# Rewriting the prologue of a hybrid attention block: raw memory rows transposed, loads in homes of their own, norm weight read from PSUM

## What is computed

```
hn    = rmsnorm(x, g_norm)                     # (1024, 1024)
proj  = hn @ w_in                              # columns aq ak av ag bq bk bv bg mq mg
a_out = sliding-window attention with sinks (aq, ak, av)
b_out = rmsnorm(differential attention (bq, bk, bv, lambda), subln_g) * (1 - lam_init)
memn  = rmsnorm(mem, g_mem)                    # (256, 1024)
kv    = memn @ w_mem_kv                        # 4 heads of keys, 4 of values
m_out = attention of mq over kv
h     = x + concat(a_out*silu(ag), b_out*silu(bg), m_out*silu(mg)) @ w_out
y     = rmsnorm(h, g_final)
```

## Time and profile before

| | us |
|---|---|
| median of 3 runs | 725.78 (725.2 to 725.81) |
| the profiled execution, device time | 726.04 |
| its span in the trace | 724.2 |

### The profile page before, as it was taken

How to read it: one execution, slowest core, us unless ns; L and a number is a source line. 1 busy time by engine, 2 the same in 40 slices (tenths; PEclk the granted TensorE clock), 3 DMA queues, 4 the chain that set the end, 5 groups by cost and what they waited for, 6 DMA issues and landing times.

```text
span 724.2 us, 11962 instructions
## 1 busy us (share of the span) xinstructions
PE 710.4 (98%) x3908; PEld 593.9 (82%) x3908; DVE 427.7 (59%) x916; ACT 311.9 (43%) x720; POOL 236.3 (33%) x204
## 2 busy tenths in 40 slices
PE   7999999999999999999999999999999999999996
PEld 7888788888888888888888888888888887888885
DVE  5884345776774577768357776835776686422231
ACT  5771333545544354554434545443454563212210
POOL 3564132324423232442323244232324452322210
PEclk9999999999999999999999999999999999999999
DMA  8663121111024101102400110241130266514211
GB/s 266 205 192 72 29 59 31 30 30 31 1 97 106 29 29 29 29 0 93 110 29 29 29 29 0 91 113 30 30 96 25 63 196 201 170 58 123 72 62 41
DMA packets 79400, 53.56 MB, mean 74 GB/s; under 512 B 36096, under 2 KB 71936, under 8 KB 79360
## 3 DMA queue, kind: packets, MB, share of 16 engines
q1 hardware_dynamic: 79360, 53.10, 25.6%
HBM read 44.18 MB, written 8.91 MB: 73 GB/s over the span
## 4 chain that ended last, share of the span: by engine, by line
PE 88%; issue 4%; DVE 2%; POOL 2%; ACT 1%; DMA 1%; SPq 0%; DVEq 0%; POOLq 0%; ACTq 0%
PE acc L1316 18%; PE acc L1317 17%; PE acc L1318 17%; PE score L1316 3%; PE score L1317 3%; PE score L1318 3%; PE score L1444 3%; PE trans L1317 3%; PE trans L1316 3%; PE trans L1318 3%; PE score L1446 3%; PE trans L1465 2%; POOL w_lo L815 2%; PE score L1522 2%; PE mixo L1317 2%
## 5 line engine op out<-in xcount | busy, mean ns | idle before, releaser
L1316 PE MATMUL acc<-x_hi,w_hi 128*128 128x512 f32 x544 | 216.3, 398 | 0.1
L1317 PE MATMUL acc<-x_lo,w_hi 128*128 128x512 f32 x544 | 212.5, 391 | 0.0
L1318 PE MATMUL acc<-x_hi,w_lo 128*128 128x512 f32 x544 | 212.2, 390 | 0.0
L815 POOL TENSOR_TENSOR w_lo<-w_raw,w_hi 128x512 fp32r<-128x512 f32 x86 | 113.8, 1345 | 190.3 <-ACT w_hi L555 190.3
L1318 PEld LDWEIGHTS acc<-x_hi,w_lo 128*128 128x128 f32 x544 | 102.1, 188 | 22.2
L1316 PEld LDWEIGHTS acc<-x_hi,w_hi 128*128 128x128 f32 x544 | 102.3, 188 | 21.5 <-issue 1.8
L1317 PEld LDWEIGHTS acc<-x_lo,w_hi 128*128 128x128 f32 x544 | 102.4, 188 | 18.2
L672 ACT ACTIVATE logits<-logits,stats_b 128x256 f32<-128x256 f32 (+3 forms) x64 | 52.6, 824 | 46.8 <-DVE stats_b L1121 46.8
L1113 DVE CUSTOM_DVE_ANT_0 logits<-score,b_bias 128x512 f32<-128x512 f32 (+1 forms) x96 | 53.8, 599 | 22.1 <-PE score L1446 19.2
L555 ACT ACTIVATE w_hi<-w_raw 128x512 fp32r<-128x512 f32 x86 | 49.4, 624 | 27.4 <-PE acc L1318 20.0
L681 ACT ACTIVATE p_hi<-trans 128x512 fp32r<-128x512 f32 x56 | 32.5, 595 | 63.2 <-PE trans L1465 38.9
(11 more groups left out here) (191 smaller groups left out, 1340.9 us busy)
## 6 DMA issues: line engine op xcount, KB each, us to landing
w_raw<-in_w_in SPq DMA_DIRECT2D x68, 256.0 KB, 3.4
mixed<-gates SPq DMA_DIRECT2D x9, 512.0 KB, 4.3
mix_raw<-mixed SPq DMA_DIRECT2D x8, 576.0 KB, 5.6
w_raw<-in_w_mem_kv SPq DMA_DIRECT2D x16, 256.0 KB, 4.0
logits<-in_x SPq DMA_DIRECT2D x8, 512.0 KB, 4.6
wo_raw<-in_w_out SPq DMA_DIRECT2D x8, 512.0 KB, 6.5
x_res<-in_x SPq DMA_DIRECT2D x8, 512.0 KB, 3.4
out_y<-y_row SPq DMA_DIRECT2D x16, 256.0 KB, 2.1
```

What stands on the lines that cost most here:

```text
L815: last = pool.tensor_tensor(w_lo[:, slot, cols], w_raw[:, slot, cols], w_hi[:, slot, cols].bitcast(F32), ALU.subtract)
L1316: pe.matmul(out, a_hi, b_hi, start=start, stop=False, skip_group_check=True)
L1317: pe.matmul(out, a_hi, b_lo, start=False, stop=False, skip_group_check=True)
L1318: return pe.matmul(out, a_lo, b_hi, start=False, stop=stop, skip_group_check=True)
```

## The change

All of it lies in the prologue; the head loop and the end are as before.

- The memory rows are no longer scaled before they are transposed. TensorE transposes them raw (8 + 8 transposes). The norm weight is applied when the transposed banks are split, where it is one number per partition (ScalarE with a scale column, VectorE L964 becoming a multiply-and-subtract, 8 operations of 256 columns each). The rows' 1/rms is applied when the products come out of PSUM: `mem_tile` multiplies by mem_rstd, which is made by two 128-wide ScalarE operations, two transposes and one copy.
- Norm weights: two DMAs of 8 rows x 512 B instead of two spread ones of 512 KB. g_mem is transposed into columns (gain_cols). g_norm is spread to all partitions in PSUM by 8 matmuls in plain float32 with a picking matrix, into two banks (gain_spread), and stays there.
- x rows are scaled in place, in pairs of blocks, as two 512-column halves per block that read the weight from PSUM. The Newton step's operations all have one tensor operand and column scalars; before, two of the five had two tensor operands.
- Homes: 8 for x blocks, 8 for memory weight tiles (two in w_raw, two in a_v, four in the upper 256 columns of x_hi and x_lo). So SP issues, with no wait but a short one on a memset, the memory, the weights' rows, tiles 0 to 7 and x blocks 0 to 5 in one stream, in the order t0 t1 t2 x0 t3 x1 t4 x2 t5 x3 t6 x4 t7 x5, then tiles 8 and 9, x6, x7, the constants.
- Weight halves: GpSimd signals each half (`w_lo_half`), and VectorE makes the first half of tile 0. TensorE begins a tile on its first half.
- Four PSUM banks for memory products and, in part, for transpositions, where there were two. Transposes come in groups of 4 between products: none until tile 4, then 4 after each tile, the rest among tiles 8 and 9, which run in the order 8 left, 9 left, 8 right, 9 right.
- The products that nobody reads shrink from 32 + 16 + 12 to 14 + 2 + 2.
- The table work on a_bias and b_bias moves from the end of the prologue to its start.

```diff
-BUSY = (32, ((0, 512), (8, 512), (16, 512), (32, 512)), ((64, 512), (0, 516), (0, 576)))
+BUSY = (14, 2, 2)
...
 @@ SP
             sp.dma_start(mem_raw[0][:, :], mem_rows[:, 0, :]).then_inc(mem_full[0], 16)
-            sp.dma_start(g_mem_b[:, :], g_mem.partition_broadcast(P)[:, 0, :]).then_inc(gmem_full, 16)
             sp.dma_start(mem_raw[1][:, :], mem_rows[:, 1, :]).then_inc(mem_full[1], 16)
...
+            for n in range(3):
+                load_mem_tile(n)
+            for t in range(5):
+                load_row(t)
+                load_mem_tile(t + 3)
+            load_row(5)
+            sp.wait_ge(w_lo_first, 1)
+            for par, col in enumerate((AV, AK)):
+                sp.wait_ge(w_lo_done, 1 + par)
+                load_tile(w_in_v, par, col, None)
+            load_row(6)
+            load_row(7)
...
 @@ ACT, in this order
+            row_squares(mem_raw[0][:, :], 0, mem_full[0])
+            mem_bank_hi(0)
+            w_hi_half(0, 0)
+            mem_bank_hi(1)
+            w_hi_half(0, 1)
+            mem_bank_hi(2)
+            mem_bank_hi(3)
+            split_hi(1)
+            row_squares(mem_raw[1][:, :], 1, mem_full[1])
+            pair_std(0)
+            split_hi(2)
+            spread_mem_rstd()
+            row_squares(x_raw[0], 2, rows_full[0])
+            split_hi(3)
...
 @@ DVE
+                        last = dve.scalar_tensor_tensor(out=row[:, cols], in0=row[:, cols],
+                                                        scalar=row_stats[:, 2 * pair + n + 2, 6:7],
+                                                        in1=gain_spread[s], op0=ALU.mult, op1=ALU.mult)
...
+            def mem_tile(n):
+                dve.wait_ge(acc_full, n + 1)
+                out = mk_raw[:, n // 2, :] if n % 2 == 0 else mv_t[:, (n // 2) * MEM:(n // 2 + 1) * MEM]
+                dve.tensor_tensor(out, pre_acc[n % 4][:, 0:MEM], mem_rstd, ALU.mult).then_inc(acc_free, 1)
...
+            for n in range(3):
+                mem_tile(n)
+            normalise(0)
+            mem_tile(3)
+            mem_tile(4)
+            for b in range(2):
+                x_bank_lo(0, b)
+            normalise(1)
+            mem_tile(5)
+            for b in range(2, 4):
+                x_bank_lo(0, b)
+            mem_tile(6)
+            for b in range(2):
+                x_bank_lo(1, b)
+            mem_tile(7)
+            for b in range(2, 4):
+                x_bank_lo(1, b)
+            normalise(2)
+            normalise(3)
...
 @@ PE
+            for n in range(MEM_TILES):
+                mem_tile(n)
+                if n == 1:
+                    pe.wait_ge(mem_spread_made, 1)
+                    for par in range(2):
+                        last = pe.transpose(trans[:, 0, par * P:(par + 1) * P], mem_spread[:, par, :], ident[:, :])
+                    last.then_inc(mem_rstd_turned, 1)
+                if n >= 4:
+                    pair, half = divmod(n - 4, 2)
+                    for b in range(2 * half, 2 * half + 2):
+                        spread_rows(pair, b)
...
+            shared_half(8, 0, range(KT))
+            for b in range(2):
+                spread_rows(2, b)
+            shared_half(9, 0, first)
+            for b in range(2, 4):
+                spread_rows(2, b)
+            shared_half(9, 0, (4, 5))
+            for b in range(2):
+                spread_rows(3, b)
+            shared_half(9, 0, (6, 7))
+            for b in range(2, 4):
+                spread_rows(3, b)
+            shared_half(8, 1, first)
```

More of the change, by code:

```diff
@@ L580, in _ @@
[L580 to L601, removed]
@@ L958, in _ @@
[L958 to L965, removed]
@@ new lines, in normalise @@
+            def normalise(pair):
+                if pair == 0:
+                    dve.wait_ge(gain_spread_made, 1)
+                pair_rstd(pair + 1)
+                for n in range(2):
+                    row = x_raw[2 * pair + n]
+                    for s in range(2):
+                        cols = slice(s * HALF, (s + 1) * HALF)
+                        last = dve.scalar_tensor_tensor(out=row[:, cols], in0=row[:, cols],
+                                                        scalar=row_stats[:, 2 * pair + n + 2, 6:7],
+                                                        in1=gain_spread[s], op0=ALU.mult, op1=ALU.mult)
+                last.then_inc(rows_done, 1)
@@ new lines, in x_bank_lo @@
+            def x_bank_lo(pair, b):
+                out = slice(2 * b, 2 * b + 2), slice(pair * 2 * P, (pair + 1) * 2 * P)
+                if pair == 3 and b == 0:
+                    dve.wait_ge(w_lo_done, MEM_TILES)
+                n = 4 + 4 * pair + b
+                dve.wait_ge(t_hi, n + 1)
+                dve.tensor_tensor(x_lo[:, out[0], out[1]], pre_t[n].rearrange("p (k n) -> p k n", k=2),
+                                  x_hi[:, out[0], out[1]].bitcast(F32), ALU.subtract).then_inc(t_free, 1)
@@ new lines, in mem_tile @@
+            def mem_tile(n):
+                if n >= 4:
+                    pe.wait_ge(acc_free, n - 3)
+                for k in range(KT):
+                    if k == 0:
+                        pe.wait_ge(*((w_lo_half, n) if n else (w_lo_first, 1)))
+                    if k == KT // 2:
+                        pe.wait_ge(w_lo_done, n + 1)
+                    if n == 0 and k % 2 == 0:
+                        pe.wait_ge(t_free, k // 2 + 1)
+                    w = slice(k * P, (k + 1) * P)
+                    last = product(pre_acc[n % 4][:, 0:MEM], w_hi[:, n % 2, w], w_lo[:, n % 2, w], mem_hi[:, k, :],
+                                   mem_lo[:, k, :], k == 0, k == KT - 1)
+                last.then_inc(acc_full, 1)
@@ new lines, in _ @@
+            for b in range(4):
+                spread_mem(0, b)
+            keep_busy_wide(BUSY[1])
+            pe.wait_ge(gain_full, 32)
+            pe.transpose(acc[:, 0, 0:P], gain_rows, ident[:, :]).then_inc(gain_turned, 1)
+            pe.wait_ge(mem_full[1], 16)
+            for b in range(4):
+                spread_mem(1, b).then_inc(t_full, 1)
+            pe.wait_ge(gain_picked, 1)
+            for k in range(KT):
+                last = pe.matmul(gain_spread[k // 4][:, (k % 4) * P:(k % 4 + 1) * P], gain_picks[:, k, :], gain_rows,
+                                 start=True, stop=True, skip_group_check=True)
@@ L1401, in head @@
+            shared_half(8, 1, rest)
+            pe.wait_ge(const_made, 6)
+            for v in range(2):
+                spread_shared(v)
+            shared_half(9, 1, first)
+            shared_half(9, 1, rest)
+            pe.wait_ge(acc_free, 11)
+            for v in range(2, 4):
+                spread_shared(v)
             def head(h, order):
```

419 lines of the change are left out of this document (257 added, 162 removed).

## The result

| | before | after |
|---|---|---|
| median, us | 725.74 (4 runs) | 717.43 (4 runs, 717.08 to 718.01) |
| span of the profiled execution | 724.2 | 715.9 |
| first product that counts | 17.15 | 9.97 |
| head loop's first product | 77.25 | 66.93 |
| from there to the end of the span | 646.95 | 648.97 |

The ratio is 0.9885 with a 95% interval of 0.9873 to 0.9897: faster by 8.3 us, where 11.1 were forecast. The time lies in the stated range, at its upper side. The prologue ends 10.3 us earlier; 2.0 of them are gone again by the end.

The account below looks back on a forecast made before the run. TensorE was taken to bound the kernel, so the head loop starting at 66.0 instead of 77.25 saves 11.25 us: 724.2 + 1.84 - 11.25 = 714.8, median 0.26 lower, 714.6; range 712.4 to 718.8.

Parts of the forecast that it names:

- TensorE bounds, so the head loop's start decides: Whole kernel: TensorE is busy 98% of 724.2 us; the gain is how much earlier than 77.25 the head loop starts.
- the terms written for it: Prologue from tile 2 at 16.8: products and transposes 48.0, giving 64.8 without waits; 1.0 for changes; waits summing to 3.0, overlapping.
- The rest moves as a block: Head loop and end: the 646.95 us behind the loop's start stay the same length and only begin earlier.
- A loop longer than 647.4: Sign of being wrong: the span behind the head loop's first product exceeds 647.4 us instead of staying 647.
- The start: Prologue up to tile 2: earlier arrivals and half-tile splits put the first product at 9.45 and tile 2 at 16.8.
- VectorE is the tight one: Steady prologue: VectorE needs 7.5 us per pair of blocks against TensorE's 7.4; rows done at 24.7, 32.2, 43.7, 48.0.
- scalings above 0.7: Sign of being wrong: VectorE's 512-column scalings of x in the prologue take over 0.7 us, against about 0.6 forecast.
- The third wait forecast: Prologue: TensorE waits 1.0 us for the banks of pair 3.
- The rival that a scaling takes 1.1 us: Prologue: VectorE becomes the bound, 16 scalings of 1.1 instead of 0.6 cost 8 us; head loop at 72.5, 721; 7%.
- goes for good: Prologue: VectorE operations with two SBUF operands no longer stretch beside GpSimd: 2.28 instead of 1.29 a scaling, 1.23 a one-column product.
- The clock rival: Start: TensorE's step to full pace comes late, tile 0 and part of tile 1 run slowly; 0.8 to 2 us lost; 5%.
- DMA: Prologue loads: tile 7 lands by 25.6 at 333 GB/s, wanted at 31; starvation rival 4% for 720, 2% for 727.

Follow-up runs that it names:

- the trace with 128 bytes: Changed kernel with gain_cols in unused columns of stats_b (old addresses, 715.28), plus 128 bytes left free ahead of stats_b: 722.02 us.
- whole tiles: Changed kernel with old addresses and without idle products (715.06), but TensorE begins each weight tile only when both halves of its split are done: 717.22 us.

## Why the prediction was right, and where not

- **TensorE bounds, so the head loop's start decides:** right. 66.93 against 66.0. Tile 2 started at 16.61, against 16.8. But the 66.0 does not follow from the terms written for it, and part of the agreement is luck. The terms give 64.8 + 1.0 = 65.8, which leaves 0.2 us for waits that the same paragraph adds up to 3.0; with all of them it would have been 68.8. Measured were 1.15 us of waits, and 64.8 - 0.2 + 1.0 + 1.15 = 66.75 is close to the 66.93.
- **The rest moves as a block:** wrong, and this is the step that failed. It cost 2.0 us of the 2.8 that are missing. The argument looked at waits, and no new ones came; the rate itself changed, because one small allocation shifted the operands. With the old addresses the same change gives 715.28, where the forecast was 714.6. In the diff the allocation was one line, and I read it as free. A loop longer than 647.4 was among the signs of being wrong, and it came.
- **The start:** the chain was right link by link: memory block 0 at 4.13 (4.1), gain columns 7.12 (6.8), first half of weight tile 0 at 8.06 (8.1). The eight float32 products took 1.7 us to the next start (7.72 to 9.43), not 0.86, and this is a row misread: the earlier trace rows has eight instructions, but its kernel line issues four products in a turn, and each is two instructions in the trace. So the row shows 0.215 us a product, 1.7 for eight, which is what was measured. With two idle products behind them they held the first product to 9.97 instead of 9.45. I took it that tile 0 hides such a delay; the trace with 128 bytes, which has the same prologue, starts its first product at 9.41 and tile 2 at 16.04, so half a microsecond here was not hidden.
- **VectorE is the tight one:** right. The rows of the four pairs were done at 24.66, 32.24, 44.2 and 48.7, where 24.7, 32.2, 43.7 and 48.0 were forecast. Waits of 0.6 and 0.6 were measured for 1.2 and 0.8 forecast, at the same two places. A scaling is 0.66 apart, not 0.6, one microsecond more for 16, but the rows of pairs 0 and 1 were in time all the same, although scalings above 0.7 (0.74 busy) were among the signs of being wrong. The third wait forecast, 1.0 at pair 3, did not come.
- **The rival that a scaling takes 1.1 us:** it did not happen, because PSUM operands kept 0.74. But its mechanism is real: with the operand in SBUF it was 1.43, and the time 723.49, where the rival gave 721. I named the stretching as something that "goes for good" and gave it no price; it is 6 us for the scalings and 9 for the single columns, in each some 1.7 of them by TensorE's clock, which no term of the prediction has. The Trainium skill (SBUF — State Buffer, SBUF: two separate sides) states that an operation of VectorE with two SBUF inputs and one of GpSimd that reads SBUF exclude each other for the whole instruction. The maximum of 1303 ns beside a split of 1.3 us agrees with it.
- **The clock rival:** a small cost that varies, less than the 0.8 to 2 us of the rival in the changed kernel. The profiled executions of one and the same prologue differ in when the pace rises, and the start moves with it: with 128 bytes, in the changed kernel and with the old addresses the first product starts at 9.41, 9.97 and 10.71, tile 2 at 16.04, 16.61 and 17.34, the head loop at 66.62, 66.93 and 67.81. So up to 1.2 us hang on it. The addresses alone are not the reason: the kernels without idle products and with whole tiles begin with the same transposes at the same addresses, and full pace came near 9.5 us in one and near 7.5 in the other. The Trainium skill says that full speed does not engage for transposes (TensorE: Matmul & The Clock Gate, Part 4: PE-mode transpose). Two traces here disagree: in the kernel before and in the one with whole tiles full pace came while TensorE had done nothing but transposes. In the kernel without idle products it did not come in 3.7 us of them. What decides the moment stays open.
- **DMA:** no starvation. The stream ran at 329 GB/s, and no rounding of a weight tile in the changed kernel waited for its load. What I did not price is what the homes bring, with the order of issue that they allow: 4.1 us.

## What to carry to other kernels

A part that is worth nothing alone can be what a rewrite stands on: single-column operations with one tensor operand bring 0.75 us where VectorE has room and 8.9 where it bounds, beside a GpSimd that works in SBUF. When TensorE has to stand for another engine, read the granted clock of the microseconds behind the wait as well as the wait itself. After a change to the allocations compare the length and the busy time of a stretch that has the same instructions in both traces, before any gain is credited to an edit; and put small new tensors where nothing moves. Where one engine has a fixed order and bounds, look in it for short work that waits behind something late and can stand before it.

## What the runs showed of the hardware that I had not expected

- The rate of TensorE's matmuls depends on where the operands lie in SBUF: the same 3459 instructions took 646.4, 649.4, 653.0 and 653.9 us at shifts of 0, 64, 128 and 32 bytes, at a granted clock of full speed in each. The products of x with w carry it, those of wo with the mixed rows do not. Why is open.
- The pace of TensorE at the start changes from run to run and does not show in the profile's clock: the first transposes take 423 ns each and 272 later, while the page grants full speed for both, and the same two wide idle products behind the memory's transposes were busy 0.71 us in the changed kernel and 1.20 in the same kernel with the old addresses. The first product of the second came 0.74 us later (10.71 against 9.97), tile 2 0.73 and the head loop 0.88.
- TensorE's granted clock fell to 0.50 (1.2 GHz) in the prologue of two kernels, after waits of 2.12 and 3.07 us. After a wait of 2.43 us in one of these kernels, and one of 1.94 in the other, it stayed at 1.00. What decides it is not shown.
- A plain float32 product is two instructions in the trace: eight of 128 columns took 1.7 us to the next start, and four of 192 columns on half the array 0.86.
